# Split-weight slots 32 bytes longer each, feed-forward activations 96 bytes further on

## The reference

```python
for l in range(2):                                   # first_block
    x = x + 0.5 * swiglu(rms_norm(x, g1), w1, w2)    # w1: 1024 x 5632, w2: 2816 x 1024
    x = x + hybrid_mixer(rms_norm(x, g), ...)        # LRU, latent attention, conv; three gated branches
    x = x + 0.5 * swiglu(rms_norm(x, g2), w1b, w2b)
x = rms_norm(x, final)
for l in range(2):                                   # second_block
    x = x + rms_norm(hybrid_mixer_2(rms_norm(x), ...))
    x = x + rms_norm((silu(a) * b) @ w_down)         # a, b = split(conv3(h @ w_up)), same sizes
```

## The kernel before

| tensor | before | after |
|---|---|---|
| `raw` | 128 | 128 |
| `w_hi`, slots 0, 1, 2, 3 | 128, 128, 128, 128 | 128, 160, 192, 224 |
| `w_lo`, slots 0, 1, 2, 3 | 128, 128, 128, 128 | 0, 32, 64, 96 |
| `h_hi`, `h_lo` | 192 | 192 |
| `hid_hi`, `hid_lo`, `m_hi`, `m_lo` | 192 | 32 |
| `o2_hi`, `o2_lo` | 64 | 160 |
| `win_hi` | 64 | 160 |
| `win_lo` | 192 | 32 |

## Time and profile before

### The profile page before, as it was taken

The page is one execution under the profiler, slowest core; times in us unless marked ns, Lnnn a source line. Parts: engine busy times, 40 slices in busy tenths (PEclk is TensorE's granted clock), DMA queues, the critical chain, the costliest instruction groups (busy, mean ns, idle before and its releaser), DMA issues.

```text
span 2045.1 us, 39527 instructions
## 1 busy us (share of the span) xinstructions
PE 1973.3 (96%) x15240; PEld 1872.4 (92%) x15240; DVE 1391.4 (68%) x2058; ACT 1159.5 (57%) x1847; POOL 140.5 (7%) x153
## 2 busy tenths in 40 slices
PE   7999999999999999999999999989899999899998
PEld 7999988999999999988999999877899987679997
DVE  5765788667655665788666656874898477648963
ACT  5444675564445434676565445665676448556753
POOL 1053100010000001100010001000200010002000
PEclk9999999999999999999999999999999999799999
DMA  5555444455555545443455544530354543313643
GB/s 213 205 171 189 153 148 141 153 200 192 185 170 199 199 159 192 162 150 125 154 183 206 189 169 161 176 134 21 127 203 167 203 141 125 124 42 124 226 157 111
DMA packets 53533, 329.80 MB, mean 161 GB/s; under 512 B 5936, under 2 KB 6704, under 8 KB 27952
## 3 DMA queue, kind: packets, MB, share of 16 engines
q1 hardware_dynamic: 53424, 328.34, 45.9%
HBM read 327.27 MB, written 1.05 MB: 161 GB/s over the span
## 4 chain that ended last, share of the span: by engine, by line
PE 67%; DVE 9%; issue 9%; ACT 6%; DVEq 3%; DMA 3%; POOLq 3%; POOL 1%; ACTq 0%; SPq 0%
PE bank L662 17%; PE bank L663 17%; PE bank L664 17%; PE bank L715 5%; DVE w_lo L641 4%; DMA raw<-in_w 3%; ACT w_hi L602 2%; PE bank L1656 1%; PE bank L1672 1%; PE bank L677 1%; PE bank L679 1%; PE bank L1111 1%; PE bank L686 1%; DVE x L1946 1%; PE bank L1673 1%
## 5 line engine op out<-in xcount | busy, mean ns | idle before, releaser
L641 DVE TENSOR_TENSOR w_lo<-raw,w_hi 128x2048 fp32r<-128x2048 f32 (+3 forms) x348 | 673.7, 1940 | 332.4 <-ACT w_hi L602 313.7
L662 PE MATMUL bank<-h_hi,w_hi 128*128 128x256 f32 x2704 | 768.6, 284 | 11.8 <-DVE w_lo L641 5.0
L663 PE MATMUL bank<-h_lo,w_hi 128*128 128x256 f32 x2704 | 756.4, 280 | 0.0
L664 PE MATMUL bank<-h_hi,w_lo 128*128 128x256 f32 x2704 | 756.2, 280 | 0.0
L602 ACT ACTIVATE w_hi<-raw 128x2048 fp32r<-128x2048 f32 (+2 forms) x346 | 560.7, 1624 | 138.2 <-DMA raw<-in_w 112.1
L662 PEld LDWEIGHTS bank<-h_hi,w_hi 128*128 128x128 f32 x2704 | 508.9, 188 | 16.6 <-issue 11.1
L663 PEld LDWEIGHTS bank<-h_lo,w_hi 128*128 128x128 f32 x2704 | 508.5, 188 | 1.2
L664 PEld LDWEIGHTS bank<-h_hi,w_lo 128*128 128x128 f32 x2704 | 509.0, 188 | 0.0
L662 PE MATMUL bank<-hid_hi,w_hi 128*128 128x256 f32 x1056 | 295.3, 280 | 0.0
L663 PE MATMUL bank<-hid_lo,w_hi 128*128 128x256 f32 x1056 | 294.8, 279 | 0.0
L664 PE MATMUL bank<-hid_hi,w_lo 128*128 128x256 f32 x1056 | 294.8, 279 | 0.0
(11 more groups left out here) (337 smaller groups left out, 2950.3 us busy)
## 6 DMA issues: line engine op xcount, KB each, us to landing
raw<-in_w SPq DMA_DIRECT2D x198, 1024.0 KB, 4.8
raw<-in_w SPq DMA_DIRECT2D x96, 704.0 KB, 4.0
raw<-in_w SPq DMA_DIRECT2D x52, 768.0 KB, 4.2
raw<-in_w SPq DMA_DIRECT2D x8, 512.0 KB, 3.9
raw<-in_w SPq DMA_DIRECT2D x4, 576.0 KB, 3.7
x<-in_x SPq DMA_DIRECT2D x1, 1024.0 KB, 4.9
out<-x SPq DMA_DIRECT2D x4, 256.0 KB, 2.4
const<-in_const SPq DMA_DIRECT2D x1, 548.0 KB, 5.6
```

What stands on the lines that cost most here:

```text
L641: dve.tensor_tensor(w_lo[:, s % SPLIT_SLOTS, 0:n], raw[:, s % RAW_SLOTS, 0:n], w_hi[:, s % SPLIT_SLOTS, 0:n].bitcast(F32), ALU.subtract).t ...
L662: pe.matmul(out, hi, x_hi, start=start, stop=False, skip_group_check=skip)
L663: pe.matmul(out, hi, x_lo, start=False, stop=False, skip_group_check=skip)
L664: return pe.matmul(out, lo, x_hi, start=False, stop=stop, skip_group_check=skip)
```

## The change

Each slot of `w_hi` and `w_lo` gets 8 more numbers (32 bytes) that nothing uses, so that slot n begins n times 32 bytes further by remainder, and `w_lo` as a whole 128 bytes further. Together this is 256 bytes, so that everything behind, up to `sin2`, keeps its remainder. `offset_hid` grows from 96 to 192 bytes: `hid_hi` and all that shares the space behind it (the tensors of both mixers) move by a further 96 bytes. Every instruction, its sizes, its order and its waits stay as they were; only addresses differ.

```diff
+SLOT_WORDS = 16 * P + 8
...
-        w_hi = sbuf("w_hi", [P, SPLIT_SLOTS, 16 * P], F32R)
-        w_lo = sbuf("w_lo", [P, SPLIT_SLOTS, 16 * P], F32R)
+        w_hi = sbuf("w_hi", [P, SPLIT_SLOTS, SLOT_WORDS], F32R)
+        w_lo = sbuf("w_lo", [P, SPLIT_SLOTS, SLOT_WORDS], F32R)
         sbuf("offset_h", [P, 16])
...
-        sbuf("offset_hid", [P, 24])
+        sbuf("offset_hid", [P, 48])
```

## The result

The change made the kernel slower: 2056.86 us as the median of 9 runs (2054.05 to 2061.33), beside 2047.88 us for the kernel before in 9 runs on the same chip (2043.81 to 2052.82). The ratio is 1.0046, with a 95% interval of 1.0034 to 1.0057. I had forecast 2026 us. The time lies inside the range of 1995 to 2077, on the other side of the kernel before: the change of 0.46% is small, but its interval leaves 1.0 out.

A forecast was written before the change was run, and what follows sets the result against it. TensorE was taken as the bound, its span a count of matmuls times their step; 2045.1 - 23 us for TensorE's reads, all else 0, gave 2022 us of span, and 2026 us as the median, range 1995 to 2077.

The forecast's parts named there:

- both bounds of the term: TensorE's reads in split matmuls: all steps at 113.6 ns give -46 us, all at 120.0 give +26 us.
- Splits, loads and waits for them: VectorE and ScalarE splits and the weight loads: no gain or loss from the new addresses, 0 us.
- the writers: Writes into one slot while TensorE reads another: no collision with its reads, so spreading the slots gains nothing there.
- one nanosecond is worth 11.3 us: Split matmuls on TensorE: each nanosecond of step counts 11.3 us over 11,280 matmuls.
- What is freed is kept: Feed-forward stretches: TensorE is always busy, and a 5.45 us unit still covers the 4.8 us load, so savings stay.
- A state that is shaken at every unit of 5.65 us has many chances to fall into the level that holds: Split matmuls: remainders changing by 32 bytes each unit would let steps enter the lasting 113.6 ns level more often.
- half of the matmuls at 113.6: -23 us: Value taken for TensorE's reads: half of the split matmuls step at 113.6 ns, saving 23 us.
- The good level: Split matmuls' faster step of 113.6 ns, against 117.6 nearly everywhere; claimed to hold once entered at remainders 192 and 64.
- rows 6 and 7: Profile stretches moving o2 (22 steps in 2.50 us) and h (7 in 0.79 us), cited for the 113 ns level.
- Rival one: Split matmuls: remainder changes inside each group of three cost, step about 119.3 ns, +18 us, 2067 us; chance 0.33.
- A slot with a mean above 122 ns: Sign of an altogether wrong prediction: distance 0 puts both streams into lasting collision in one slot of four.
- Rival two: Split matmuls: a stretch's start sets its level, not addresses; feed-forwards keep 117.6 ns, 2049 us within 3; chance 0.20.

The follow-up runs named there:

- all_plus64: Kernel before with offset_h 128 bytes longer, slots unchanged: weights stand 64 bytes above h and hid instead of 64 below; 2019.40 us, ratio 0.9878.
- lo_half_turn: Kernel before with w_lo moved 128 bytes from w_hi's remainder, every slot alike: distances -64 high, +64 low for h and hid; 2048.73 us, ratio 1.0013.
- slots_alike: Kernel before with slots 32 bytes longer, w_lo at w_hi's remainder: distance changes from unit to unit, not within a group; 2050.86 us, ratio 1.0029.

## Why the prediction was wrong

**What held.** TensorE's step bounds the kernel, its excess depends on how weights and moved activations stand to each other, and both bounds of the term (113.6 and 120.0) are levels that the runs then showed over whole feed-forwards. Splits, loads and waits for them were at zero, and stayed there; no effect of the writers was needed to explain the result. That one nanosecond is worth 11.3 us held for TensorE's own time, not for the span. "What is freed is kept" is refuted by all_plus64, which kept 14.3 us of 27.7.

**The step that failed** is "A state that is shaken at every unit of 5.65 us has many chances to fall into the level that holds", and with it "half of the matmuls at 113.6: -23 us". The good level isn't what any distance falls into. Over whole feed-forwards the runs show it at +64 alone; shorter runs show it also at -64, seldom, and with the two in alternation, often. Of the eight pairs of slot and weights that `h` has after the change one is at +64 and one at -64, and they stand in the same group, where they change off. lo_half_turn gives that very pair to every slot. `hid` then stands at 118.89 with no stretch at 113. Of the steps of `h` half are near 113 in the mixers, as I had assumed for all, but only 6% in the feed-forwards, where two thirds of them are. slots_alike, which keeps the shaking and drops the alternation, wins clearly at one slot of one tensor only. The measured value of the term is +0.9 ns for `h` and +1.1 for `hid` in place of -2.1. My sign came from taking rows 6 and 7, both at a distance of 64, as news of addresses in general; `o2` in rows 6 stands at +64, though the prediction says that every load stands at -64. That the time lies inside the range is no merit of the forecast: the range reached that far because of the rivals.

**Rival one** had the sign and the place: fewer than 845 matmuls in 100 us (841, 844), steps that differ inside the group. Its price of +1.6 for every group was too high, and its cause is only half of it. Its ground was weaker than I took it to be: the 120.0 ns of the compression are those of the second layer. The first layer runs the same instructions at the same addresses, and at a granted clock of 1.00, at the good level:

```profile
1329.48 0.28 PE L723 MATMUL bank<-w_lo,win_hi 128*128 128x256 f32 x1
...
1330.50 0.28 PE L723 MATMUL bank<-w_lo,win_hi 128*128 128x256 f32 x1
```

These are 9 steps in 1.02 us, 113 ns; the whole compression has a mean of 117.0. Worked out with the table: the levels of the single distances, high weights counted twice, give 118.3 for `h` and 118.4 for `hid`, some +0.7 and +0.6 over before, above all because slots at 0 and +160 (the remainder of -96) stand at 120. What is left, +0.2 and +0.5, is the change of distance inside the group, a mean over slots in which it costs (slot 1 of `h` +1.7, by the pair above) and slots in which it gains (slot 2 of `h`, 0 and +128: 119.0, where the single levels give 119.6; slot 1 of `hid`, +128 and 0: 118.2 for 119.2). This remainder is a difference of means and not the result of a run that has the alternation by itself in every slot. A slot with a mean above 122 ns doesn't occur; the worst has 120.73.

**Rival two**, that nothing happens, is out: ten of the thirteen changed kernels, counting the change itself, lie outside 1.0 by their intervals. What it said on starts is nevertheless true wherever there are two levels at the same addresses: over whole feed-forwards at +64, where the level is settled within ten steps, and in short runs at -64, in the compression and in lo_half_turn. So my question was put too simply: the runs show that addresses decide which levels there are, and that a stretch takes one of them near its start.

**A reading that was loose.** The mean of the stretch and the step of the timeline agree to 0.4 ns (117.9 and 117.5), not to 0.2, and the timeline gives its 12 steps to about 1 ns. The conclusion on the writers doesn't rest on it: the long stretches hold 117.78 or 113.34 through all spells of VectorE and ScalarE.

The rule of the Trainium skill ("SBUF — State Buffer", section "Who interferes with whom") that TensorE's reads have independent ports and wait for no one does not describe this: with no other difference than addresses, the step goes from 113.3 to 120.0 ns. Likewise the Trainium skill's page "TensorE: Matmul & The Clock Gate", section "Back-to-back issue gap", gives 262 cycles at the full clock for 256 columns, as the spacing of matmuls without the weight loads; worked out at 2.4 GHz this is an estimate of 109 ns. The split matmuls have a weight load each, and none of their stretches comes below 113.3.

**What stays open.** Why the distance matters. That the two reads disturb each other is argued and not shown; what may stand behind the 256 bytes no run tells, and that the pattern repeats by 256 was assumed in naming remainders and not tried. What in the first steps of a stretch at +64 picks 113.3 or 117.8. Why the short runs of the mixers take the good level where the feed-forwards don't. Whether it is the distance or the weights' place at 144 that takes the good level from +48 and +80. The levels at distances that no kernel had by themselves (+112, -16, +16 and others).

## What to carry to other kernels

When an engine streams two operands back to back, read the step between starts in each stretch and ask whether it is constant and the same everywhere: if it has several levels at one clock, relative addresses are a lever, and one line of padding can be worth over 1% (-24.7 us here, all_plus64) or cost as much (+21.4 at -96). Read the waits too: part of what a shorter step gives goes to them, and to the lower clock behind them. Try one distance at a time, the same for all operands of a group, before spreading anything: spreading mixes bad levels in, and adds a cost of its own at each change. And don't carry a level that was seen at one distance to distances that no row shows, nor one that was seen in a short run to a long one.

## What the runs showed of the hardware that was not expected

A float32r matmul of 256 columns has steps from 113.3 to 120.0 ns at a granted clock of 1.00, by the distance of weights and moved operand alone. At +64 it has two, each stable over more than 1,200 matmuls (113.34 and 117.78); at +48 and +80, with the weights at 144, the lower one is gone. Alternating between two distances can be slower than either of them (116.7 and 117.3 alone, 118.8 mixed), and in two slots it was faster than their mean (119.0 for 119.6, 118.2 for 119.2). The same instructions at the same addresses can run at 113 ns in one layer and at 120 in the other (the compression of the kernel before).
